# The small table of the overflow blocks moved behind the first expert's gate product

## The reference

```
group_logits = xt @ rg_w + rg_b                  # (512, 4), softmax, argmax -> grp
expert_logits = xt @ re_w + re_b                 # (512, 32); those of grp: top 2
gate = p_grp * softmax(top_val)
for each expert e, for its tokens:  ys = (silu(x @ w_gate[e]) * (x @ w_up[e])) @ w_down[e]
out[token] += gate * ys
x = x + out;  return rmsnorm(x, final_norm_g)
```

## Time and profile before

| | us |
|---|---|
| median of 3 runs (1810.66 to 1812.04) | 1811.15 |
| span of the profiled execution | 1807.8 |
| TensorE busy in the span | 1706.9 |
| VectorE busy | 1194.1 |
| ScalarE busy | 903.2 |
| GpSimd busy | 110.7 |

### The profile page before, as it was taken

How to read it: one execution, slowest core, us unless ns; L and a number is a source line. 1 busy time by engine, 2 the same in 40 slices (tenths; PEclk the granted TensorE clock), 3 DMA queues, 4 the chain that set the end, 5 groups by cost and what they waited for, 6 DMA issues and landing times.

```text
span 1807.8 us, 18646 instructions
## 1 busy us (share of the span) xinstructions
PE 1706.9 (94%) x7626; PEld 1312.4 (73%) x7626; DVE 1194.1 (66%) x1310; ACT 903.2 (50%) x997; POOL 110.7 (6%) x139
## 2 busy tenths in 40 slices
PE   5999998999999999999899999979999999999994
PEld 1767664666778888888688767868888888888882
DVE  7533546687454344343569585489999898989893
ACT  6424444443332323232533204368787877787872
POOL 0000003000000000000000130011010101010100
PEclk8999999999989999999899998979999999999997
DMA  9114451002213222322122100259999999999983
GB/s 379 50 74 168 186 188 46 1 1 93 93 47 116 94 96 90 113 83 84 47 93 73 50 18 29 71 221 376 363 374 380 375 357 367 360 372 369 378 315 151
DMA packets 54523, 322.79 MB, mean 179 GB/s; under 512 B 12577, under 2 KB 13089, under 8 KB 17826
## 3 DMA queue, kind: packets, MB, share of 16 engines
q1 hardware_dynamic: 42480, 305.81, 44.9%
q0 software_dynamic: 9216, 8.42, 1.4%
q10 hardware_dynamic: 2738, 7.33, 1.0%
HBM read 325.70 MB, written 20.97 MB: 192 GB/s over the span
## 4 chain that ended last, share of the span: by engine, by line
PE 85%; DVE 8%; ACT 3%; DMA 2%; issue 1%; POOL 0%; SPq 0%; DVEq 0%; POOLq 0%; ACTq 0%
PE ps L517 33%; PE ps L1259 18%; PE ps L1286 10%; PE ps L623 3%; DVE wlo L1914 2%; PE ps L1148 2%; PE ps L843 2%; PE ps L1245 2%; DVE scr L2194 1%; ACT whi L1347 1%; PE ps L909 1%; PE ps L656 1%; PE ps L988 1%; PE ps L946 1%; DMA xT<-in_x 1%
## 5 line engine op out<-in xcount | busy, mean ns | idle before, releaser
L1914 DVE TENSOR_TENSOR wlo<-raw,whi 128x2048 fp32r<-128x2048 f32 x284 | 642.6, 2284 | 196.5 <-ACT whi L1347 196.3
L1347 ACT ACTIVATE whi<-raw 128x2048 fp32r<-128x2048 f32 x284 | 538.1, 1913 | 198.6 <-PE ps L517 103.2
L517 PE MATMUL ps<-hH,whi 128*128 128x512 f32 x576 | 230.0, 399 | 8.3 <-DVE wlo L1914 8.3
L517 PE MATMUL ps<-hL,whi 128*128 128x512 f32 x576 | 227.2, 394 | 0.0
L517 PE MATMUL ps<-hH,wlo 128*128 128x512 f32 x576 | 227.2, 394 | 0.0
L1259 PE MATMUL ps<-whi,xH 128*128 128x512 f32 x512 | 203.5, 398 | 0.0
L1259 PE MATMUL ps<-whi,xL 128*128 128x512 f32 x512 | 201.2, 393 | 0.0
L1259 PE MATMUL ps<-wlo,xH 128*128 128x512 f32 x512 | 200.6, 392 | 0.0
L517 PEld LDWEIGHTS ps<-hH,whi 128*128 128x128 f32 x576 | 107.9, 187 | 38.3 <-DVE wlo L1914 12.1
L517 PEld LDWEIGHTS ps<-hH,wlo 128*128 128x128 f32 x576 | 107.9, 187 | 26.6
L517 PEld LDWEIGHTS ps<-hL,whi 128*128 128x128 f32 x576 | 107.9, 187 | 26.0 <-issue 0.5
(11 more groups left out here) (469 smaller groups left out, 2646.2 us busy)
## 6 DMA issues: line engine op xcount, KB each, us to landing
raw<-in_experts SPq DMA_DIRECT2D x192, 1024.0 KB, 7.3
raw<-in_streamed SPq DMA_DIRECT2D x92, 1024.0 KB, 4.9
xT<-in_x SPq DMA_DIRECT2D x1, 2048.0 KB, 17.2
h_scratch<-hN ACTq DMA_DIRECT2D x4, 512.0 KB, 2.6
Y<-y_scratch SPq DMA_DIRECT2D x4, 512.0 KB, 7.8
Y<-y_scratch ACTq DMA_DIRECT2D x4, 512.0 KB, 8.1
out<-xN SPq DMA_DIRECT2D x4, 512.0 KB, 2.6
ctxT<-in_ctx SPq DMA_DIRECT2D x1, 1024.0 KB, 18.7
```

Source lines behind the costliest of these rows:

```text
L517: ins = e.matmul(o, l, r, start=(i == 0), stop=(i == len(prs) - 1))
L1347: e.activation(u.hi, u.raw, ACT.Copy).then_inc(*p.inc("hi", n, on="hi"))
L1914: e.tensor_tensor(u.lo, u.raw, u.hi.bitcast(F32), ALU.subtract).then_inc(*p.inc("lo", n, on="lo"))
```

## The change

On TensorE, `table(1, 16, Rty)` moves from the end of the route stage to behind the two gate halves of expert 0. On VectorE, everything behind the second `R1` is split in three functions. `second_blocks` (from `e8` to `Rty`) is called between `turn_x(0)` and `turn_x(1)`; `block_experts` (`ovt` to `ovi`) after the conversions of `U_E["g", 0]` and before `gates()`; `second_numbers` in the first turn of the loop, after its first conversion. SyncE's load of `FIFTH` waits for the last index too.

```
@@ pe_program, route stage
         for m in range(4, 8):
             token_major(m)
-        table(1, 16, Rty)
@@ pe_program, moe stage
         half_mm(0, "g", 0)
         half_mm(0, "g", 1)
+        table(1, 16, Rty)
         for x in range(NEXP):
@@ dve_program, route stage
         TT(R1, b8(iot, 128), p12.unsqueeze(2).broadcast_to([P, 8, 128]), ALU.is_equal)
-        p.wait_ge(*p.own())
-        for k in range(2):
-            TT(e8[:, k], rowb(ob, 32), O12[:, k], ALU.mult)
...
+        def second_blocks():
+            p.wait_ge(*p.own())
+            for k in range(2):
+                TT(e8[:, k], rowb(ob, 32), O12[:, k], ALU.mult)
...
+            TT(Rty[:, :, 0:8], ob8, valt.unsqueeze(2).broadcast_to([P, 8, 8]), ALU.mult)
+            TT(Rty[:, :, 8:16], ob8, valy.unsqueeze(2).broadcast_to([P, 8, 8]), ALU.mult, "R", 1)
+
+        def block_experts():
+            j8 = C("j7").unsqueeze(2).broadcast_to([P, 8, 32])
+            TT(ovt, b8(ob), j8, ALU.is_le)
+            TT(ovm, b8(oi), j8, ALU.is_gt)
...
+            copy(ovi[:, :], ovf[0:1, :], p.inc("ovi"))
+
+        def second_numbers():
+            numbers("tt", 1, ps["tab", 1].t[:, 0:7], 32, idt)
+            numbers("ty", 1, ps["tab", 1].t[:, 8:15], 32, idy)
@@ dve_program, moe stage
+        p.wait_ge(*p.own())
         p.stage("moe")
...
         turn_x(0)
+        second_blocks()
         turn_x(1)
         for n in U_E["g", 0]:
             use(n)
+        block_experts()
         gates()
         for x in range(NEXP):
             r = x % 2
             use(U_E["u", x][0])
+            if x == 0:
+                second_numbers()
             p.wait_ge(*done("act", "sig", x))
@@ sp_program, load(n)
             if n == FIFTH:
+                p.wait_ge(*done("dve", "idty", 1))
                 p.wait_ge(*done("dve", "gk"))
                 p.wait_ge(*done("act", "dd"))
```

More of the change, by code:

```diff
@@ L2594, in dve_program @@
         TT(R1, b8(iot, 128), p12.unsqueeze(2).broadcast_to([P, 8, 128]), ALU.is_equal)
[L2595 to L2625, removed]
+        def second_blocks():
+            p.wait_ge(*p.own())
+            for k in range(2):
+                TT(e8[:, k], rowb(ob, 32), O12[:, k], ALU.mult)
+            p.wait_ge(*p.own())
+            e.tensor_reduce(b12, e8.rearrange("p k i c -> p (k i) c"), AX.X, ALU.add).then_inc(*p.inc())
+            p.wait_ge(*p.own())
+            TT(b12, b12, q12, ALU.add)
+            p.wait_ge(*p.own())
+            TT(b12, b12, u12, ALU.mult)
+            p.wait_ge(*p.own())
+            TS(b12, b12, -1.0, None, ALU.add)
+            j88 = b8(C("j7"), 8)
+            p.wait_ge(*p.own())
+            TT(ob8, j88, b12.unsqueeze(2).broadcast_to([P, 8, 8]), ALU.is_equal)
+            p.wait_ge(*p.own())
+            TT(Rty[:, :, 0:8], ob8, valt.unsqueeze(2).broadcast_to([P, 8, 8]), ALU.mult)
+            TT(Rty[:, :, 8:16], ob8, valy.unsqueeze(2).broadcast_to([P, 8, 8]), ALU.mult, "R", 1)
@@ new lines, in block_experts @@
+        def block_experts():
+            j8 = C("j7").unsqueeze(2).broadcast_to([P, 8, 32])
+            TT(ovt, b8(ob), j8, ALU.is_le)
+            TT(ovm, b8(oi), j8, ALU.is_gt)
+            p.wait_ge(*p.own())
+            TT(ovt, ovt, ovm, ALU.mult)
+            p.wait_ge(*p.own())
+            TT(ovt, ovt, b8(iota), ALU.mult)
+            p.wait_ge(*p.own())
+            e.tensor_reduce(ovf[:, 0:8], ovt, AX.X, ALU.add).then_inc(*p.inc())
+            copy(ovf[:, 8:16], oi[:, 31:32].broadcast_to([P, 8]), p.inc())
+            p.wait_ge(*p.own())
+            copy(ovi[:, :], ovf[0:1, :], p.inc("ovi"))
```

## The result

| | before | after |
|---|---|---|
| median of 20 runs, us | 1810.26 (1805.05 to 1812.22) | 1814.37 (1812.50 to 1815.91) |
| ratio to before | | 1.0028, 95% interval 1.0021 to 1.0034 |
| span of the profiled execution, us | 1807.8 | 1812.7 |

The change makes the kernel slower by 0.28% by the ratio on record (5.1 us), and by 4.1 us (0.23%) by the two medians. The forecast was 1815.35 us, slower, with a range of 1812.4 to 1817.4.

A forecast was written before the change was run, and what follows sets the result against it. TensorE bounds the kernel, never idle over most of the expert loop, so entry shifts reach the end; 0 + 0 + 3.3 + 0.9 = +4.2 us on span 1807.8 gives 1812.0, plus 3.35 to the median: 1815.35, range 1812.4 to 1817.4.

The forecast's parts named there:

- Start of the transposes, gain 0: Entry of the expert loop: token transposes still start near 1193.46, now waiting for expert 0's gather; gain 0, bound 5.2 us.
- Rival A: Not slower: tokens land earlier once TensorE is free for them, gaining 5.2 us against 4.2, hence 1810.1 us; 5%.
- No help from the table for the clock: Before the transposes: TensorE idling instead of doing the table does not delay the clock's rise; 0, bound 0.9 us.
- The table free on TensorE: Table behind the gate product takes 0.94 us at full clock, inside TensorE's wait for `ac`: 0 by itself.
- `second_blocks` covered: Between expert 0's token turns: its 2.2 us end before the gate product does, and pushed conversions stay covered: 0.
- VectorE's train, +3.3: VectorE ahead of `ac`: `block_experts` (2.32 us) and `second_numbers` (1.02 us) find no idle time; `ac` 3.3 us later.
- The clock behind the longer stall, +0.9: TensorE's 3.5 us idle before `turn_a(0)` drops the clock; half rate loses 1.5 to 2.5 us, 0.71 covered; +0.9 taken.
- The marks: Signs in the profile: transposes within 0.3 us of 1193.46, `ac` near 1214.6, a clock dip, `down(0)` at 1221 to 1223.
- The sum: Whole kernel: 0 + 0 + 3.3 + 0.9 = +4.2 us on the span, median 1815.35 us.

The follow-up runs named there:

- the two holds: Kernel before, and changed kernel, each with SyncE's weight loads from expert 1's first gate half on waiting for the first two gathers: ratios 1.0004 and 0.9995.
- blocks_twice: Changed kernel with the arithmetic of `block_experts`, all but the last copy, done twice in its new place: 1816.26 us (1 run).
- numbers_late: Changed kernel with `second_blocks` and `block_experts` back in VectorE's wait for the tokens and `second_numbers` behind `aL` of expert 0: 1809.71 us, ratio 1.0000.
- after_hold: Changed kernel with SyncE's weight loads from expert 1's first gate half on waiting for the gathers of experts 0 and 1: 1809.70 us, ratio 0.9995.
- best2: best with `second_blocks` moved back between `turn_x(0)` and `turn_x(1)`: 1805.68 us, ratio 0.9975 to the kernel before.
- fill: Changed kernel with TensorE doing expert 1's first gate half twice, 12 more matmuls, to fill its stall: 1813.82 us, ratio 1.0019 to the kernel before.
- blocks_early: Changed kernel with `second_blocks` and `block_experts` back in VectorE's wait for the tokens: 1809.85 us, ratio 1.0000 to the kernel before.
- best: best_nohold plus SyncE's weight loads waiting for the first two gathers: 1804.12 us, ratio 0.9966 to the kernel before.
- best_nohold: Changed kernel with VectorE's parts in its waits or behind `aL`, and ScalarE's sigmoid table loaded while waiting for tokens: 1809.55 us, ratio 0.9996 to before.

## Why the prediction was right

- **Start of the transposes, gain 0**: right, 9.26 for 9.20 us. That the loads ahead cause it is shown by the two holds. Rival A would have decided from 4.2 us of earlier landing on, with 5.2 as its bound; the holds give 4.9, but only after an edit the change does not have. In blocks_twice the first tokens landed 2.6 us earlier without any such edit, so the landing is less fixed than I took it to be.
- **No help from the table for the clock**: right, the clock rose at about 1200, 4.9 us after the transposes began (before 5.1).
- **The table free on TensorE**: right, 0.95 us (forecast 0.94), and numbers_late shows it.
- **`second_blocks` covered**: right; it ended at about 1200.6, before the table's turn at 1204.84, and the pushed conversions met no waiting TensorE. The cover holds even with the tokens 4.9 us earlier: in after_hold TensorE's only waits up to `down(0)` are for the gather and for `ac`. It breaks in best2, where `block_experts` stands ahead of the conversions too (0.73 us for `wlo`).
- **VectorE's train, +3.3**: right in mechanism, measured 3.09. `block_experts` took 2.32 as forecast, the indices 0.94 instead of 1.02, and `gates()` with the gap behind it shrank from 1.51 to 1.27 us, since VectorE no longer comes to that conversion before ScalarE's part is done (about 1209.1 before, with VectorE starting at 1209.16; about 1210.7 after, with VectorE starting at 1212.85). The train ahead of them began 0.07 later; 2.32 + 0.94 - 0.24 + 0.07 is the 3.09. The removal of the parts brings back the old `ac`, the doubling of one lengthens the stall by its length.
- **The clock behind the longer stall, +0.9**: it fell and came back as said, but cost 0.45. It was low for some 3.0 us behind TensorE's restart. That made the stretch from `turn_a(0)` to `down(0)` 5.45 us long, where fill took 4.29 without its last wait; 1.16 us are lost, and 0.71 of them lay in the old slack. The forecast had 1.6 for that loss. The agreement in size is not to be trusted in any case: after_hold paid 1.70 for a stall of the same length, blocks_twice 1.27 for a longer one. Whether the execution or the other kernel makes that difference is not shown.
- **The marks**: `down(0)` at 1222.90 lies in the 1221 to 1223 that I named, but 1.54 us of it is the later issue of the gather; counted from the issue it is 37.10, where the forecast meant 37.7 (1222.0).
- **The sum**: +4.2 forecast, 3.53 in the traces, 4.1 between the medians, 3.8 to 6.2 by the ratio's interval. The absolute forecast, 1815.35, was 0.98 above the measured median. 0.89 of that is the base: the three runs of the kernel before had a median of 1811.15, the twenty have 1810.26. The distance of 3.35 us from span to median does not hold for one execution: each run is 1.8 to 1.9 us longer than its own span, and the other 1.5 us say that the profiled execution of the kernel before was a quick one.
- **Open**: why the medians tell slightly more than the 3.5 us of the traces. A dip of the clock as long as in after_hold, in executions that were not profiled, would do it; no profile of the changed kernel shows one. Between profiles the stretch from `down(0)` to the end, where all kernels do nearly the same work, varied from 587.3 to 590.9 us, and the start of the entry by 3.1 us. Part of the first goes with the clock near the end of the kernel: over that stretch it was low for some 25.6 us in the profiles before and after, and for 16.9 and 17.2 us in blocks_early and best, which have the shortest stretches (587.3 and 587.9); numbers_late (21.9 us low, 589.9 us) does not fit. That blocks_early's median is not above that of before, though its `down(0)` is 1.2 us later, is of the same size as this scatter.

## What to carry to other kernels

When an instruction block is taken off a wait, look for what else that wait was hiding: here a DMA landed in the same 0.1 us, and VectorE used the wait for work that had to go somewhere. The work that VectorE did while TensorE waited for the gather was free; the same work 16 to 20 us later, in a train with a gap of 0.15 us, cost nearly its full length. To profit, move both limits at once: shorten the transfer (hold back the loads ahead of it) and keep the helper's work in its idle times. Then look again at what was put into those idle times, for they have become shorter: the table load that was free in best_nohold held up `xH` in best2.

## What the runs showed of the hardware

- A gather issued just before two 1 MB weight loads landed 9.2 us after its issue, and 4.3 us with the loads held back. The Trainium skill ("DMA: Bandwidth & Descriptors", section SWDGE vs HWDGE vs iDMA) describes a round-robin between the two kinds of queue. In six of the seven profiles without the hold the gather came out behind the loads (8.9 to 9.2 us). In blocks_twice, with the same code up to there, it landed at 6.6 us and the second load came later, 8.2 us after its issue instead of 7.2; that one profile is the way the rule has it, the others are not. What decides it is open. The second load (its issue starts some 1.7 us behind that of the gather) in the kernel before, then in blocks_twice:

```profile
raw<-in_experts SPq DMA_DIRECT2D x1, 1024.0 KB, 7.2
```
```profile
raw<-in_experts SPq DMA_DIRECT2D x1, 1024.0 KB, 8.2
```

- Held behind the first two gathers, the weight loads delay the next two in their turn: they landed 9.3 and 7.9 us after issue in after_hold (5.7 and 3.8 in the changed kernel), without harm, since they are wanted much later.
- After a stall of 3.3 us the clock was at its 1.2 GHz level for some 3.4 us in one kernel and some 6.8 us in another; the net cost was 0.45 and 1.70 us. It fell 2.9 us after the last matmul in the first, 2.2 us in the second. With twelve matmuls of no use put in, and the stall down to 0.55 us, it held at 2.4 GHz.
